# Moving the expert biases' products behind the first gate/up half, and the final norm's row load behind the attention

## The reference, cut to what matters

```
def moe(x2d, w_r, b_r, w_gu, b_gu, w_dn, b_dn):
    logits = (x2d @ w_r + b_r)
    top_v, top_i = lax.top_k(logits, TOP_K)
    gates = jax.nn.softmax(top_v, axis=-1)
    ...
        h = xb @ w_gu[e] + b_gu[e]
        g = jnp.minimum(h[:, ::2], SWIGLU_LIMIT)
        lin = jnp.clip(h[:, 1::2], -SWIGLU_LIMIT, SWIGLU_LIMIT)
        a = g * jax.nn.sigmoid(SWIGLU_ALPHA * g) * (lin + 1.0)
        return a @ w_dn[e] + b_dn[e]
    ...
    return jnp.einsum('tk,tkd->td', gates.astype(y.dtype), y)

        x = x + g2 * moe(...)
    return rmsnorm(x, final_g)
```

## Time and profile before

| | us |
|---|---|
| median of 3 executions | 1627.58 |
| lowest and highest of them | 1626.79, 1627.83 |
| the profiled execution, its own time | 1625.93 |
| its span, first to last instruction | 1623.9 |
| PE busy in it | 1560.0 (96%) |

### The profile page before, as it was taken

The page is one execution under the profiler, slowest core; times in us unless marked ns, Lnnn a source line. Parts: engine busy times, 40 slices in busy tenths (PEclk is TensorE's granted clock), DMA queues, the critical chain, the costliest instruction groups (busy, mean ns, idle before and its releaser), DMA issues.

```text
span 1623.9 us, 22528 instructions
## 1 busy us (share of the span) xinstructions
PE 1560.0 (96%) x9460; PEld 934.3 (58%) x9460; DVE 556.9 (34%) x1083; ACT 437.1 (27%) x885; POOL 29.6 (2%) x41
## 2 busy tenths in 40 slices
PE   6999999999999999999999999999899999999998
PEld 5886773333333333334434343444399988899986
DVE  3858431111111111101101111111255574468774
ACT  3436431011101101101101101110345553356553
POOL 0210000000000000000000000000010100000000
PEclk9999999999999999999999999999999999999999
DMA  9517679999999999999999999999945533434530
GB/s 389 211 52 312 270 275 397 412 435 430 433 432 433 433 430 433 428 432 431 431 430 433 428 433 429 431 427 424 423 158 189 165 131 139 172 140 171 193 130 26
DMA packets 28519, 526.60 MB, mean 324 GB/s; under 512 B 3235, under 2 KB 4387, under 8 KB 6772
## 3 DMA queue, kind: packets, MB, share of 16 engines
q1 hardware_dynamic: 26816, 520.52, 77.0%
q0 software_dynamic: 1024, 3.15, 0.9%
q10 hardware_dynamic: 596, 1.71, 0.3%
HBM read 524.28 MB, written 1.08 MB: 324 GB/s over the span
## 4 chain that ended last, share of the span: by engine, by line
PE 73%; DMA 19%; DVE 5%; ACT 1%; issue 1%; POOL 0%; SPq 0%; DVEq 0%; ACTq 0%; POOLq 0%
PE ps L691 71%; DMA ring<-in_w_down 18%; DMA ring<-in_first 2%; PE ps L838 1%; DVE ring_r L1858 1%; PE ps L1033 0%; PE ps L1026 0%; PE ps L1255 0%; DVE mx L1976 0%; ACT arena L1686 0%; DVE arena L1926 0%; DVE arena L1925 0%; ACT w_high L1419 0%; DVE ring_r L2215 0%; DVE arena L1936 0%
## 5 line engine op out<-in xcount | busy, mean ns | idle before, releaser
L691 PE MATMUL ps<-ring,arena 128*64 128x512 f32 (+1 forms) x3840 | 708.6, 533 | 23.8 <-DMA ring<-in_w_down 15.1
L691 PEld LDWEIGHTS ps<-ring,arena 128*64 128x64 f32 (+1 forms) x3840 | 236.0, 132 | 441.1 <-issue 405.8
L691 PE MATMUL ps<-arena 128*128 128x128 f32 (+8 forms) x1732 | 302.0, 407 | 11.7 <-DVE arena L2245 4.7
L691 PEld LDWEIGHTS ps<-arena 128*128 128x128 f32 (+3 forms) x1732 | 174.3, 176 | 139.9 <-issue 121.8
L691 PE MATMUL ps<-arena_r,w_high 128*128 128x256 f32 x1360 | 247.8, 285 | 0.0
L2139 DVE TENSOR_SCALAR arena<-ps 128x512 f32<-128x512 f32 x32 | 22.1, 691 | 571.3 <-PE ps L691 571.3
L691 PEld LDWEIGHTS ps<-arena_r,w_high 128*128 128x128 f32 x1360 | 212.2, 192 | 2.9 <-issue 1.7
L691 PE MATMUL ps<-arena_r,ring_r 128*128 128x256 f32 x680 | 192.4, 283 | 0.0
L2215 DVE TENSOR_TENSOR ring_r<-ring,w_high 128x1024 fp32r<-128x1024 f32 x120 | 142.3, 1220 | 94.8 <-ACT w_high L1655 94.4
L1592 ACT ACTIVATE arena<-ps 128x256 f32<-128x256 f32 x32 | 12.3, 383 | 450.7 <-PE ps L1026 450.7
L1655 ACT ACTIVATE w_high<-ring 128x1024 fp32r<-128x1024 f32 x120 | 121.3, 1053 | 34.6 <-PE ps L691 32.6
(11 more groups left out here) (222 smaller groups left out, 1093.1 us busy)
## 6 DMA issues: line engine op xcount, KB each, us to landing
ring<-in_w_gate_up SPq DMA_DIRECT2D x62, 4096.0 KB, 20.1
ring<-in_w_down SPq DMA_DIRECT2D x29, 4096.0 KB, 18.8
ring<-in_second SPq DMA_DIRECT2D x32, 2048.0 KB, 8.1
ring<-in_first SPq DMA_DIRECT2D x17, 2048.0 KB, 14.8
ring<-in_w_down SPq DMA_DIRECT2D x12, 1024.0 KB, 12.2
ring<-in_w_gate_up SPq DMA_DIRECT2D x8, 1024.0 KB, 8.4
arena<-in_memory SPq DMA_DIRECT2D x4, 1024.0 KB, 8.4
ring<-in_first SPq DMA_DIRECT2D x4, 512.0 KB, 11.3
```

What stands on the lines that cost most here:

```text
L691: return nc.tensor.matmul(out_, lhsT, rhs, start=start, stop=stop, **kw)
```

## The change

On PE the four products of `add_biases` move from ahead of the expert biases and the first gate/up half of expert 0 to behind that half. The first half now waits only for the first half of the gathered tokens. On SP the load of `final_row` moves from behind the read of the count (where it waited for `bias_mm`) to directly behind the wait for the attention's last value product, and gets another place in `arena` (12288 instead of 15360). The semaphore `bias_mm` is gone.

```diff
-AT_G2D, AT_G2, AT_GROW, AT_DIAG = 18944, 20480, 15360, 24320
+AT_G2D, AT_G2, AT_GROW, AT_DIAG = 18944, 20480, 12288, 24320
...
             sp.wait_ge(pv_mm, N_AT)
+            sp.dma_start(final_row, io["rows"][:, 0, :]).then_inc(rows_in, 16)
             load_memory(2)
             sp.wait_ge(kvw_in["v"], 16)
             load_memory(3)
...
             count = sp.value_load(most_i[0:1, 0:1], min_val=0, max_val=T)
-            sp.wait_ge(bias_mm, 1)
-            sp.dma_start(final_row, io["rows"][:, 0, :]).then_inc(rows_in, 16)
             stream()
...
                 for half in range(2):
-                    last = mm(ps[:, 4 + 2 * t + half, :], gates_t[:, P * t:P * t + P],
+                    mm(ps[:, 4 + 2 * t + half, :], gates_t[:, P * t:P * t + P],
                               b_dn[0:N_EXPERTS, 512 * half:512 * half + 512], False, False, skip_group_check=True)
-                if t:
-                    last.then_inc(bias_mm, 1)
...
                 gather(0, 2 * SLOTS)
                 gather(1, 2 * SLOTS, 3)
+                pe.wait_ge(bgu_in, 16)
+                biases(0)
+                gathered(0, False)
+                filled_pair(0, 1)
+                gate_up(0, 0, 0, True)
                 add_biases(0)
                 add_biases(1)
-                pe.wait_ge(bgu_in, 16)
-                biases(0)
                 gathered(0, True)
-                filled_pair(0, 1)
-                gate_up(0, 0, 0, True)
                 filled_pair(1, 1)
```

More of the change, by code:

```diff
@@ L308, in build @@
                                                     sem("f_lo_set"))
-        kv_mm, kv_act, x1_mm, bias_mm = sem("kv_mm"), sem("kv_act"), sem("x1_mm"), sem("bias_mm")
+        kv_mm, kv_act, x1_mm = sem("kv_mm"), sem("kv_act"), sem("x1_mm")
         kvw_in = {"k": sem("keys_in"), "v": sem("values_in")}
```

## The result

The changed kernel takes 1629.93 us in the median of 22 executions (1626.55 to 1633.2), the kernel before 1627.56 (1625.94 to 1629.33). The ratio is 1.0016, with a 95% interval of 1.0010 to 1.0022: 2.4 us slower, where +0.2 was predicted, and above the predicted range, which ended at 1629.5.

What follows compares the result with a forecast made beforehand. The prediction took the weight stream to be bound by PE's request at 285.53 us. Its terms summed 0 + 0.2 + 0 + 0 + 0 = +0.2 us, from 1627.58 to 1627.8 us, range 1625.3 to 1629.5.

Steps and rivals of the forecast that it cites:

- What bounds the kernel: Expert loop: weight transfers run at their ceiling from 302 us; PE sets when the stream runs without a hole.
- the anchor: Weight request at 285.53 us, after expert 0's down product; its lateness leaves a 2.5 us hole, and moving it moves the end.
- The earlier first load helps nothing: Requests: first quarter load goes out at 238.6 instead of 242.11 us, absorbed by the later hole; 0, bounds -4.7 and 0.
- Row load: Load of final_row issued at 187.2 us: its delay to SP and the bias load stays hidden; 0, bounds 0 and +9.1.
- Changes of array shape: PE around the moved bias products: three changes instead of two, +0.2 us, bounds 0.1 and 0.3.
- Products: PE: the same 8 bias passes move behind the first gate/up half; later work keeps its place, 0 us.
- my rivals: Earlier start reaches the end, 1624.1 to 1622.9 us (0.07); SP reaches the stream late, 1627.8 us; moved load delays routing (0.03).
- the sign that it names itself: Prediction wrong if the request at 285.53 us moves over 0.5 us either way, or stays and the end moves.
- The slower rival: Moved row load at 187.2 us delays the expert down biases and routing: up to 1636.8 us, +0.56%; chance 0.03, with its like.

Runs made afterwards that it cites:

- full_rows: Changed kernel with 128 instead of 32 rows of weights in the four bias products, the added rows zeroed; 1627.70 us, ratio 1.0003 to the kernel before.
- before_again: The kernel before, unchanged, run again to see its granted clock beside its times; 1627.32 us.
- row_only: Changed kernel without its part on PE: only the row load moves, PE keeps the order of before; 1627.26 us, ratio 0.9999 to the kernel before.
- after_again: The changed kernel, unchanged, run again on the chip of the split runs; 1628.93 us, ratio 1.0015 to the kernel before.
- pe_only: Changed kernel with the row load back in its old place on SP, without the wait; 1630.44 us, ratio 1.0012 to the kernel before.
- between: Changed kernel with the four bias products between the expert biases and the first gate/up half; 1629.26 us, ratio 1.0018 to the kernel before.
- late: Changed kernel with all four bias products behind the second gate/up half of expert 0; 1628.16 us, ratio 1.0011 to the kernel before.
- split_mid: Changed kernel with two bias products back behind the gather, the other two between the gate/up halves; 1626.55 us, ratio 1.0000 to the kernel before.
- spread: Changed kernel with one bias product behind each block of four steps of the first gate/up half; 1627.91 us, ratio 1.0005 to the kernel before.
- old_place_more_32: Changed kernel with PE's order of before, plus eight unread 32-row passes behind the bias products; 1634.21 us, ratio 1.0047 to the kernel before.

## Why the prediction was wrong, point by point

- *What bounds the kernel.* Right. The new landings are 12.4, 13.4 and 14.5 us behind 277.84, 288.96 and 297.54, that is 290.2, 302.4 and 312.0: 12.1 us apart ahead of the anchor and 9.7 behind it, so the hole ahead of the anchor is there as before, and none behind it. A shift of PE reached the end nearly one for one, 3.43 us at the anchor and 3.1 in the span. One reading beside it was off: the slices above 420 GB/s are the ninth to the 29th of 40.6 us each, so they begin at 325 us and end at 1177, not 243 and 1140. Nothing in the sum hangs on it.

```profile
ring<-in_w_gate_up SPq DMA_DIRECT2D x1, 4096.0 KB, 12.4
...
ring<-in_w_down SPq DMA_DIRECT2D x1, 4096.0 KB, 13.4
```

- *The earlier first load helps nothing.* Right: 238.41 us, 3.7 earlier, and no gain. full_rows, without the fall behind the products, shows it alone: against before_again, whose clock falls at 231 to 235 us as well, its first quarter goes out 3.3 us earlier (240.52 against 243.78), and its anchor 0.5 us later (287.73 against 287.20).
- *Row load.* Right: row_only is the same as before. In the changed kernel the expert down biases landed after 7.5 us instead of 6.8, and VectorE took them at 199.40, without a wait:

```profile
arena<-in_b_down ACTq DMA_DIRECT2D x1, 128.0 KB, 7.5
```

- *Changes of array shape.* Right in size: the first is 242.50 to 243.45, 0.95 for two steps of 0.43, +0.09. In full_rows, with the same split, the anchor stands 56.29 us behind the start of the gather (287.73 - 231.44), in before_again 56.13 (287.20 - 231.07): +0.16 for the whole split, where 0.2 was forecast.
- **The step that failed** is in *Products*: "Everything PE does after that keeps its place. Term: 0." I priced the moved passes by their number and the step of 0.43 us, and took it that the steps behind them keep theirs. What the runs show in its place is a term for the fall of the clock behind passes with 32 rows of weights: 3.4 us in the profile of the changed kernel, next to nothing in its fastest executions (1626.55 us at the least), and 2.4 us in the medians, or 2.2 against full_rows. None of my rivals was this one, though the windows of before give PE's granted clock for every stretch, and it falls to 0.57 in 222 to 225 us while PE is busy for 3.00 of 3.00 us. The prediction says nothing of it. By the sign that it names itself, a move of the request at 285.53 by more than 0.5 us, it is wrong: the request moved by 3.43.
- *The slower rival* was of the right sign for another reason, which row_only rules out.

What stays open is where the line runs between products that bring a fall and those that do not. The runs only put cases in order. No fall was seen behind two products among 64-column steps, nor behind four right after the gather; it was seen behind four among 64-column steps in each of the five profiles that have them so (the changed kernel, after_again, pe_only, between, late), and behind the four with eight passes more, after the gather and between the halves. Most of these are one profile each. Why the changed kernel has no loss in some executions is not shown, since none of those was profiled. The mean clocks account for (0.9934 - 0.9926) x 1627 = 1.3 us of the 2.5 us by which the means differ; that the rest is the same cause follows from full_rows, where it is gone as well, but not from the clocks.

## What to carry to other kernels

Where work moves on TensorE, ask what share of the array it uses and what its new neighbours use, and read the granted clock of that stretch in the profile, not only busy time: a busy engine can lose half its speed. Where the clock falls, keep products with few rows of weights apart (split_mid, spread), or put a few of them right behind dense ones (before, while sixteen passes there were too many in old_place_more_32), or give them zeroed rows, which cost no time here. And before starting a stream of loads earlier, look for the last hole in it: in this kernel only the request behind that hole counted.

## What was not expected of the hardware

With PE busy in 4.00 of 4.00 us, eight passes (four products) of 32x128 weights and 512 columns among steps of 128x64 were followed by the 1.2 GHz level, for a loss of 3.4 us; the same eight with 128 rows were not. At full clock the 32-row passes take the same 0.43 us as those with 128 rows (243.99 to 244.42 us in the changed kernel, 246.10 to 246.53 in full_rows), so their few rows show in the clock and not in the step.
